# Row minima carried from score unit to score unit, a key copy moved from VectorE to ScalarE, and rotary rows turned later

## The reference, cut to what matters

```
latent  (A): s = (q_nope . k_nope + q_rope . k_rope) * scale, causal, softmax, times v
             sample group: 2048 cached rows through a page table, in latent form
dilated (B): softmax over three dilated windows, merged by their denominators
             sample group: a window buffer of 2048 keys and values
both    : p = exp(s - max(s)) / sum(exp(s - max(s))),  o = p @ v
```

## Time and profile before

| | |
|---|---|
| median of the runs | 1998.89 us |
| the profiled execution | 1998.15 us, span 1996.6 us |
| PE busy | 1777.9 us, 89% of the span |
| DVE, ACT, POOL busy | 896.7, 652.3, 571.5 us |
| granted TensorE clock, mean | 0.941 |
| chain that ended last | 39% PE, nearly all in the gated MLP |

### The profile page before, as it was taken

One profiled execution on the slowest core, in us unless ns is written; L12 is line 12 of the kernel. 1 busy time (PEld: TensorE's weight loads), 2 busy tenths in 40 slices (PEclk: granted clock), 3 DMA queues, 4 the chain that ended last, 5 costly groups with the idle time before them and its releaser, 6 DMA issues. The chain is left out here.

```text
span 1996.6 us, 27887 instructions
## 1 busy us (share of the span) xinstructions
PE 1777.9 (89%) x9955; PEld 1549.3 (78%) x9955; DVE 896.7 (45%) x1858; ACT 652.3 (33%) x1321; POOL 571.5 (29%) x533
## 2 busy tenths in 40 slices
PE   3999968888996878886969969999999999999997
PEld 2888857777875766776757859889889888888885
DVE  5333325566664666565743412332332333333335
ACT  4222115556554544544432212112211211211212
POOL 0000003554552446564630012212212311321211
PEclk9999988899987988998979979999999999999999
DMA  7222133233106553543334127488578659668632
GB/s 237 102 101 92 70 98 87 57 89 89 45 6 160 145 155 94 162 114 110 92 128 153 27 78 144 117 156 127 129 138 135 137 121 161 123 126 177 107 74 94
DMA packets 156106, 227.41 MB, mean 114 GB/s; under 512 B 31111, under 2 KB 129032, under 8 KB 149576
## 3 DMA queue, kind: packets, MB, share of 16 engines
q1 hardware_dynamic: 153134, 159.39, 26.8%
q0 software_dynamic: 2880, 66.85, 20.7%
HBM read 201.12 MB, written 91.93 MB: 147 GB/s over the span
## 5 line engine op out<-in xcount | busy, mean ns | idle before, releaser
L2168 DVE TENSOR_TENSOR acc<-f_dp,acc 128x512 f32<-128x512 f32 x198 | 136.5, 691 | 197.9 <-PE f_dp L2249 197.9
L2039 POOL TENSOR_TENSOR f_gl<-f_graw,f_gh 128x1024 fp32r<-128x1024 f32 x22 | 52.9, 2404 | 378.8 <-ACT f_gh L2083 378.8
L2249 PE MATMUL f_dp<-f_dh,f_ah 128*128 128x512 f32 x396 | 155.4, 392 | 4.6 <-DVE f_al L2199 4.0
L2249 PE MATMUL f_dp<-f_dl,f_ah 128*128 128x512 f32 x396 | 154.9, 391 | 0.0
L2249 PE MATMUL f_dp<-f_dh,f_al 128*128 128x512 f32 x396 | 154.7, 391 | 0.0
L2182 DVE SCALAR_TENSOR_TENSOR f_gc<-f_gp,f_coef,f_gc 128x832 f32<-128x832 f32 x44 | 47.7, 1085 | 233.4 <-ACT f_lasts L2103 230.5
L523 PE MATMUL zp<-win_h,xT_h 128*128 128x512 f32 (+1 forms) x288 | 112.7, 391 | 0.0
L1550 POOL TENSOR_TENSOR w_vl<-w_v,w_vh 96x2048 fp32r<-96x2048 f32 (+3 forms) x32 | 111.2, 3486 | 2.0
L523 PE MATMUL zp<-win_l,xT_h 128*128 128x512 f32 (+1 forms) x288 | 111.4, 387 | 0.0
L523 PE MATMUL zp<-win_h,xT_l 128*128 128x512 f32 (+1 forms) x288 | 111.3, 386 | 0.0
L768 POOL TENSOR_SCALAR l_pr<-l_pr,l_rden 128x128 f32<-128x128 f32 (+7 forms) x64 | 47.0, 746 | 172.1 <-DVE l_rden L868 172.1
(11 more groups left out here) (343 smaller groups left out, 4886.6 us busy)
## 6 DMA issues: line engine op xcount, KB each, us to landing
out_s_win_k<-in_state_win_k POOLq DMA_DIRECT2D x10, 3264.0 KB, 43.5
out_s_win_v<-in_state_win_v POOLq DMA_DIRECT2D x10, 3264.0 KB, 46.0
w_k<-in_state_win_k SPq DMA_DIRECT2D x16, 768.0 KB, 7.2
w_v<-in_state_win_v SPq DMA_DIRECT2D x16, 768.0 KB, 5.6
f_graw<-in_w_gate SPq DMA_DIRECT2D x22, 512.0 KB, 4.4
f_uraw<-in_w_up SPq DMA_DIRECT2D x22, 512.0 KB, 4.9
f_draw<-in_w_down SPq DMA_DIRECT2D x11, 1024.0 KB, 34.5
m_c<-in_cache_kv_latent SPq DMA_DIRECT2D x128, 64.0 KB, 1.8
```

Source lines behind the costliest of these rows:

```text
L2039: nc.gpsimd.tensor_tensor(w_lo[n][:], w_raw[n][:], w_hi[n][:].bitcast(F32), ALU.subtract)\
L2168: nc.vector.tensor_tensor(a, dp[h][:], a, ALU.add).then_inc(S["d_add"], 1)
L2249: last = nc.tensor.matmul(dp[h][:], a[:, c, t * P:(t + 1) * P], w[:, c, h * 512:(h + 1) * 512], start=(c == 0 and j == 0), stop=(c == 1 an ...
```

## The change

1. Row minima: the second and later score unit of a row takes the first unit's minimum as the start value of its own (a scalar operand read from SBUF in place of a constant), so the last unit's result is the whole row's. The small minimum instructions (864, 1233, 1626) go, and ACT's exponential waits for the last score unit itself; for the prompt, for that of its own head. DVE waits for its own earlier unit first.
2. In the dilated stage the copy across the key halves becomes an ACT instruction in an event of its own, `swap`, right behind `prep`; ACT waits for DVE's two subtractions.
3. In the latent sample side `rT(g)` moves from in front of `cT(g)` to behind `s(g-1)`, the exponential and `rows(g+1)`.
4. The order is held for each engine apart (`turns_of`), with empty lists of shifts, and some waits that followed from the one order are now written out on ACT (in `prep`, `cT`, `rT`, `k_turn`).

```diff
 prep(n, what, f):
+            if self.kind == 1 and what == 1:
+                E.append((("swap", n, f), 0))
 PromptSide.scalar, prep:
+            if n:
+                last = n * PT - 1
+                self.ring.ready(act, ("score", last - 4, 1, 0) if what == 0 and f == 0 else ("score", last, 1, f))
+        elif e[0] == "swap":
+            _, n, f = e
+            cols = slice(f * 512, f * 512 + 512)
+            self.ring.done(act, ("prep", n, 1, 0, f))
+            nc.scalar.copy(self.kl[0:HD, :, cols], self.kh[HD:P, :, cols]).then_inc(S["k_ok"], 1)
 PromptSide.scalar, exp:
-                if last:
-                    act.wait_ge(S["min"], k // PT * 4 + s - 3)
-                else:
-                    self.ring.done(act, ("score", k, h, 0))
+                self.ring.done(act, ("score", k, h, last))
 PromptSide.vector:
-            if what == 1:
-                self.ring.done(dve, e)
-                nc.vector.tensor_copy(lo[0:HD, :, cols], hi[HD:P, :, cols]).then_inc(S["k_ok"], 1)
...
+            low = HUGE
+            if c:
+                self.ring.done(dve, ("score", k, h, 0))
+                low = self.nm[:, k % 2, 0, h:h + 1]
...
-                nc.vector.tensor_tensor(m[:, 2, :], m[:, 0, :], m[:, 1, :], ALU.min).then_inc(S["min"], 1)
 LatentSide.plan:
             if b < B:
-                E.append((("rT", g), 0.45))
                 E.append((("cT", g), 0.45))
             if 1 <= g <= 4 * B:
                 E.append((("s", g - 1), 0.95))
             if h == 0 and 1 <= b <= B:
                 E.append((("exp", b - 1), 0))
-            if b < B and g + 1 < 4 * B:
-                E.append((("rows", g + 1), 0))
+            if b < B:
+                if g + 1 < 4 * B:
+                    E.append((("rows", g + 1), 0))
+                E.append((("rT", g), 0.45))
 LatentSide.vector (WindowSide alike, over its three units):
+                self.ring.done(dve, ("s", e[1] - 1) if h else ("s_new", b))
+                low, at = self.st[rows, h:h + 1], h + 1
...
-            nc.vector.tensor_reduce(self.st[rows, 5:6], self.st[rows, 0:5], AX.X, ALU.min).then_inc(S["min"], 1)
```

More of the change, by code:

```diff
@@ L573, in __init__, with plan @@
         self.use, self.by, self.free, self.high = {}, [], {}, {}
[L575 to L588, removed]
+    def plan(self, turns, sides):
+        used = {eng: [(e, sides[i].bank_use(e)) for i, e in turns[eng] if sides[i].bank_use(e)]
+                for eng in ("tensor", "scalar", "vector")}
+        self.by = [e for e, _ in used["tensor"]]
+        self.use = {e: u for u, e in enumerate(self.by)}
+        self.high = {e: n + 1 for n, e in enumerate(e for e, kind in used["scalar"] if kind == "hd")}
+        self.free = {e: ("bank_a", n + 1) for n, e in enumerate(e for e, kind in used["scalar"] if kind == "a")}
+        self.free |= {e: ("bank_d", n + 1) for n, e in enumerate(e for e, kind in used["vector"] if kind != "a")}
     def take(self, pe, e):
@@ L852, in vector @@
                 tab = self.table[:, SEQ - (s + 1) * P + c0:SEQ - (s + 1) * P + c0 + w]
+            low = HUGE
+            if c:
+                self.ring.done(dve, ("score", k, h, 0))
+                low = self.nm[:, k % 2, 0, h:h + 1]
             dve.sem_inc(S["neg_go"])
             nc.vector.tensor_tensor_reduce(
-                out=self.pr[:, k % 2, h, c0:c0 + w], in0=bank[:, 0:w], in1=tab, scale=-self.scale, scalar=HUGE,
+                out=self.pr[:, k % 2, h, c0:c0 + w], in0=bank[:, 0:w], in1=tab, scale=-self.scale, scalar=low,
                 op0=ALU.add, op1=ALU.min, accum_out=self.nm[:, k % 2, c, h:h + 1]).then_inc(R["bank_d"], 1)
[L857 to L863, removed]
-                nc.vector.tensor_tensor(m[:, 2, :], m[:, 0, :], m[:, 1, :], ALU.min).then_inc(S["min"], 1)
         elif e[0] == "over":
@@ L1149, in scalar @@
             b = e[1]
-            act.wait_ge(S["min"], b + 1)
+            self.ring.done(act, ("s", 4 * b + 3))
             p = self.pr[self.half(b), :]
-            nc.scalar.activation(p, p, ACT.Exp, bias=self.st[self.half(b), 5:6], scale=-1.0,
+            nc.scalar.activation(p, p, ACT.Exp, bias=self.st[self.half(b), 4:5], scale=-1.0,
                                  accum_out=self.st[self.half(b), 6:7]).then_inc(S["exp"], 1)
@@ L1381, in weave, with turns_of @@
     return [(i, e) for _, i, e in sorted(timed, key=lambda x: x[0])]
+def turns_of(order, later):
+    return {eng: [x for _, x in sorted(((n + later.get(eng, {}).get((x[0], x[1][0]), 0), x) for n, x in enumerate(order)),
+                                       key=lambda at: at[0])]
+            for eng in ("sync", "gpsimd", "scalar", "vector", "tensor")}
+LATENT_LATER = {}
+DILATED_LATER = {}
 def latent_attention(nc, sem, io):
@@ L1398, in _ @@
         def _(sp):
-            for i, e in order:
+            for i, e in turns["sync"]:
                 sides[i].sync(sp, e)
@@ L1410, in _ @@
         def _(act):
-            for i, e in order:
+            for i, e in turns["scalar"]:
                 sides[i].scalar(act, e)
@@ L1420, in _ @@
         def _(pe):
-            for i, e in order:
+            for i, e in turns["tensor"]:
                 sides[i].tensor(pe, e)
@@ L1617, in vector @@
                 self.ring.ready(dve, ("p_turn", b - 2, 1))
+            low = HUGE
+            if u:
+                dve.wait_ge(S["s_free"], 3 * b + u)
+                low = self.st[rows, u - 1:u]
             dve.sem_inc(S["neg_go"])
```

56 lines of the change are left out of this document (27 added, 29 removed).

## The result

The changed kernel takes 1919.26 us in the median of four runs (1918.5 to 1920.26), beside 1998.87 us before (1998.83 to 1999.7): a ratio of 0.9601, 95% interval 0.9584 to 0.9618. It is 79.6 us faster. The forecast was 1972 us in a range of 1948 to 1992, so the sign was right and the size was a third of what came: 26 us of 80.

What follows compares the result with a forecast made beforehand. PE was taken as the bound, idle in both attention stages and then at half clock. Dilated minima 13, key copy 7 and clock 10, less a third, gave 20; latent 4 + 2; 1998.15 - 26 = 1972 us, range 1948 to 1992.

Steps and rivals of the forecast that it cites:

- rotary rows 4: Latent stage: moving the rotary rows wins 14.5 us of PE waits, loses 10 to a later ACT copy, net 4.
- minima 2: Latent stage: 16 small minimum instructions and 8 reductions go, winning 2 us, with ends of 0 and 8.
- with no change of the clock taken: Latent stage: the rotary rows' net 4 us was counted without any clock gain.
- The price of 1.5 us a place for the rotary copy: Latent stage: ACT's rotary copy, now behind the sample's exponential, delays PE 1.5 us in the mean at seven places, 10 us.
- I let a third return: 20 us.: Dilated stage: of 30 us won by minima, key copy and clock, other waits take back a third, leaving 20.
- Dilated minima, 13 us: Dilated stage: without separate minima exponentials start 1.5 us sooner a step, shortening PE's key-rest waits; 13 us, ends 0 and 22.2.
- Key copy, 7 us: Dilated stage: moving the key copy from DVE to ACT wins 7 us; ends 20 lost and 17.4 won.
- Start values and waits at nothing: Both attention stages: scalar start values add 0 to 8 us on DVE, nothing on the path; written-out ACT waits cost about nothing.
- (1): Rival, chance 0.17: the next wait, POOL's split or the swap, eats the freed time; nothing from the latent stage; 1988 us.
- (4): Rival, chance 0.07: POOL holds up score units with an SBUF scalar as it did the minimum; 1989 us.
- (3): Rival, chance 0.08: latent rotary copy behind the sample's exponential stops PE at seven places with half clock, 41 us lost; 2004.
- (2): Rival, chance 0.06: nothing returns and the rotary rows win in full with their clock; 1938 us.

Runs made afterwards that it cites:

- m1_minima: Changed kernel keeping only the carried minima, in both stages; rotary rows in front and key copy on DVE as before the change; 1956.07 us, ratio 0.9789.
- m2_moves: Changed kernel with all minima as separate instructions again; rotary rows stay behind and the key copy stays on ACT; 1970.84 us, ratio 0.9867.
- m4_stall: Changed kernel plus three ACT copies behind each latent sample exponential, and the dilated prompt's minima again separate two-input instructions; 1962.33 us, ratio 0.983.
- n2_late: Changed kernel with the latent sample's minimum separate again and the dilated swap moved behind the following step's first turn copy; 1923.47 us, ratio 0.9627.
- n1_reduce: Changed kernel with the prompt's minimum separate again in both stages, as a reduction reading one SBUF tensor; 1934.53 us, ratio 0.9678.
- n3_twice: Changed kernel without any key copy; DVE subtracts a second time from PSUM straight into the copied half's place; 1918.6 us, ratio 0.9595.
- n4_ctl: Kernel before the change, plus only the separate orders by engine and the waits written out on ACT; 1998.9 us, ratio 1.0002.

## Why the prediction was wrong

The sum was 26 us and the two stages gave 77. By terms:

| term | forecast | measured | difference |
|---|---|---|---|
| dilated, idle time (minima 13, key copy 7) | 20 | 25.4 | 5.4 |
| dilated, clock | 10 | 14.5 | 4.5 |
| dilated, returned by what takes its place | -10 | 0 | 10 |
| latent, idle time (rotary rows 4, minima 2) | 6 | 18.3 | 12.3 |
| latent, clock | 0 | 18.8 | 18.8 |
| sum | 26 | 77.0 | 51.0 |

**The step that failed most: the latent stage worked out "with no change of the clock taken".** It is 18.8 of the 51 us. The prediction gave the dilated stage its clock, by the 0.50 in the earlier trace rows, and then worked out the latent stage in idle time alone, though it had itself put the clock not granted there at 31 us. For the rotary rows it says so; for the latent minima the term is left out without a word. Each part alone shows the clock beside the idle time: the two fell by 5.2 and 8.8 us in m1_minima, by 8.9 and 8.9 in m2_moves. In m4_stall, where stops were added and nothing was taken away, they rose by 6.1 and 7.8. The two do not always go together: the swap of m2_moves took 9.3 us of idle time from the dilated stage and no busy time, since the time that the low level lost there was time in which PE stood idle.

**Latent idle time, 6 against 18.3.** Three things are in the 12.3 us that were missing. The rotary rows alone gave 8.9 for the net 4. Their own two waits came out near the forecast (16.9 us gone, 14.1 added, where 14.5 and 10 were taken); the rest lay in PE's waits for DVE's rests of the prompt, for which the sum had no term. The minima alone gave 5.2 for the 2, inside the ends of 0 and 8, and by another way than ACT's wait: PE's wait for POOL's rows fell by 5.3 us. The last 4.2 us came only from both together. The price of 1.5 us a place for the rotary copy was read off the stretch of the earlier trace rows, with ACT's exponential as late as it was before; another part of the same change moved that exponential, and 5.2 us were left of the 14.3. So behind the moved rotary rows the minima are worth more than in the old order: 315.8 - 296.4 = 19.4 us of the stage with the clock, of which n2_late puts 9.6 on the sample's and n1_reduce 7.8 on the prompt's.

**"I let a third return: 20 us."** Nothing returned. The wait named for it, PE's for POOL's value split, grew by 1.0 us, and no other of PE's waits in the stage by more than 0.8. The allowance of 10 us stood for no row; it was caution, set against a sum whose terms were already low.

**Dilated minima, 13 us, mis-sized.** Alone they took 16.6 us of idle and 11.9 of busy time (m1_minima). The way was as described: the two-column minimum beside POOL's subtraction, then exponentials, key copies and PE; n1_reduce prices the hold at 17.1 us and the order at 9.6. For the one wait that was priced the 13 us held: PE's wait for the key rests fell by 12.1 us of 22.2 in m1_minima and by 13.1 in the changed kernel. But the exponentials also release the turned window probabilities and the probability rests, and these waits, for which the sum had no term, fell by 4.4 and 0.7 us in m1_minima and by 7.9 together in the changed kernel.

**Key copy, 7 us: right.** 8.9 us in m2_moves, for the reason given. The Trainium skill (Perfetto Trace Analysis, Optimizing Scalar/DVE Operations) has DVE as the faster engine where a performance mode is available. The durations agree where POOL does not interfere, 687 to 690 ns on DVE in four of eight copies against 1044 on ACT; the other four took 2891 to 4817 ns beside POOL, and these decided. n3_twice adds that DVE does as well with another instruction.

**Start values and waits at nothing: right.** 63 ns a unit where 70 were allowed, no spread, and n4_ctl is level with before.

**The rivals.** (1) and (4) fell with the rows above; (3), the rotary copy behind the exponential, was there while the minima were apart (14.3 us of waits in m2_moves, of the 17 it had) and fell as the exponential came sooner. (2) was the nearest: nothing returns, the rotary rows win in full with their clock. It had 30 us for each stage, where 37.2 and 39.8 came; in the latent stage it lacked the rest of the minima's gain, of which 8.8 us are clock. Its chance of 0.06 was too low: what spoke against it, that ACT is given more to do, named no row with a wait that would take the freed time, and the earlier trace rows showed the clock.

What stays open: which single stops brought each low stretch in the dilated stage, and why the rotary rows alone shorten PE's waits for DVE's rests.

## What to carry to other kernels

Split a stage into PE's idle and busy time at a fixed count of matmuls before pricing a change: if its granted clock is below 1, an idle microsecond that goes can take a busy one with it, and this has to be asked of every stage, not only of the one whose slow stretch you looked at. What came back in these runs was half of the time in which PE was busy at the low level; low time in which it stood idle gave nothing. Price the parts of one change in the state that the other parts leave, not in the old trace: a wait read off behind an instruction is only as long as that instruction is late. And a small instruction between a result and the engine that needs it can cost by its place in the order far more than by its duration: eight reductions, 1.2 us of DVE's time, were worth 9.6 us.

## What the runs showed of the hardware

A minimum of two columns with two operands from SBUF took 974 ns in the mean beside POOL's long subtractions, the same minimum as a reduction of one operand 145 to 160 ns. In the latent stage of the kernel before, where POOL's subtractions are shorter, the two-operand form takes 230 ns in the mean: twelve at 150 to 160, and four of 225 to 872 that end with a subtraction of POOL. The Trainium skill (SBUF — State Buffer, Who interferes with whom) says that an instruction on DVE with two SBUF inputs contends with a POOL instruction that reads SBUF, and that one with at most one doesn't unless it is in a two-port mode: both minima agree. The key copy has one input and was held for up to 4817 ns; that agrees only if the copy ran in such a mode, which no run here shows. Its undisturbed 687 ns for 1024 columns, beside 688 ns for 512 in the subtraction from PSUM (n3_twice), are the double rate that would fit. A score unit that reads PSUM, a table from SBUF and now a scalar from SBUF was not held: the eight of 512 columns in the dilated stage take 741 to 751 ns, and one of 128 columns in the middle of a POOL subtraction 0.35 us (at 707.27, above). So the scalar did not count as a second input.
